# A two-layer encoder trunk on one core: the first norm on rows of x, the residual's transposes between the first products

## What is computed

```python
def rmsnorm(x, g):
    xf = x.astype(F32)
    y = xf * lax.rsqrt(jnp.mean(xf * xf, axis=-1, keepdims=True) + EPS)
    return (y * g.astype(F32)).astype(x.dtype)

# layer 0, its first lines
# u = rmsnorm(x, norm_mix[0])
a_q, a_ckv, i_q, i_k, i_w, b_qkv, b_z, b_beta, b_a = _split(u @ w_in, AB_SIZES)
```

## Time and profile before

| | us |
|---|---|
| median of three runs | 2592.58 |
| lowest and highest | 2591.0, 2593.51 |
| the profiled execution | 2587.56 |
| its span | 2585.8 |
| TensorE busy in it | 2488.4 (96%) |
| VectorE, ScalarE, GpSimd busy | 1549.3, 1008.7, 215.1 |

### The profile page before, as it was taken

How to read it: one execution, slowest core, us unless ns; L and a number is a source line. 1 busy time by engine, 2 the same in 40 slices (tenths; PEclk the granted TensorE clock), 3 DMA queues, 4 the chain that set the end, 5 groups by cost and what they waited for, 6 DMA issues and landing times.

```text
span 2585.8 us, 33956 instructions
## 1 busy us (share of the span) xinstructions
PE 2488.4 (96%) x13076; PEld 1955.7 (76%) x13078; DVE 1549.3 (60%) x2649; ACT 1008.7 (39%) x1816; POOL 215.1 (8%) x243
## 2 busy tenths in 40 slices
PE   7999999998898999999999998998999999999998
PEld 5587777875546788888888786776878888888786
DVE  6379976855544685656543546728576566553444
ACT  4323324545433343333332433428444333333333
POOL 4015533410000000000010000000000000000000
PEclk8999989999999999999999999999999999999999
DMA  5121100000003322222364341110332322336342
GB/s 174 48 74 41 41 25 10 3 34 1 1 25 121 131 74 82 83 80 82 90 225 146 133 137 41 43 39 28 96 114 82 98 66 87 94 100 234 122 159 102
DMA packets 207184, 217.54 MB, mean 84 GB/s; under 512 B 12496, under 2 KB 174304, under 8 KB 203568
## 3 DMA queue, kind: packets, MB, share of 16 engines
q1 hardware_dynamic: 204080, 196.13, 24.4%
q0 software_dynamic: 2944, 19.24, 2.1%
HBM read 172.35 MB, written 42.47 MB: 83 GB/s over the span
## 4 chain that ended last, share of the span: by engine, by line
PE 88%; DVE 6%; ACT 4%; issue 2%; POOL 0%; DVEq 0%; ACTq 0%; POOLq 0%
PE ps L333 24%; PE ps L334 24%; PE ps L335 24%; PE ps L2887 2%; PE ps L2864 1%; PE ps L2875 1%; ACT d_p L1524 1%; DVE met L2012 1%; PE ps L2251 1%; PE ps L2265 1%; PE ps L2260 1%; PE ps L1797 1%; PE ps L2304 1%; PE ps L2228 1%; PE ps L2313 1%
## 5 line engine op out<-in xcount | busy, mean ns | idle before, releaser
L322 DVE TENSOR_TENSOR wlo<-wraw,whi 128x1024 fp32r<-128x1024 f32 x152 | 186.4, 1227 | 370.0 <-ACT whi L316 369.6
L316 ACT ACTIVATE whi<-wraw 128x1024 fp32r<-128x1024 f32 x166 | 175.0, 1055 | 354.3 <-PE ps L335 337.6
L333 PE MATMUL ps<-ahi,whi 128*128 128x512 f32 x704 | 275.3, 391 | 6.5 <-DVE hT L960 4.3
L334 PE MATMUL ps<-alo,whi 128*128 128x512 f32 x704 | 273.9, 389 | 0.0
L335 PE MATMUL ps<-ahi,wlo 128*128 128x512 f32 x704 | 273.9, 389 | 0.0
L333 PE MATMUL ps<-uhi,whi 128*128 128x512 f32 x608 | 244.7, 402 | 8.2 <-DVE ulo L492 4.2
L333 PE MATMUL ps<-q_T,whi 128*128 128x512 f32 x640 | 249.2, 389 | 1.6 <-ACT upr L761 1.6
L335 PE MATMUL ps<-q_T,wlo 128*128 128x512 f32 x640 | 249.0, 389 | 0.0
L334 PE MATMUL ps<-q_T,whi 128*128 128x512 f32 x640 | 249.0, 389 | 0.0
L333 PE MATMUL ps<-q_B,whi 128*128 128x512 f32 x608 | 238.9, 393 | 2.4 <-DVE q_B L492 2.4
L335 PE MATMUL ps<-uhi,wlo 128*128 128x512 f32 x608 | 238.0, 392 | 0.0
(11 more groups left out here) (459 smaller groups left out, 4517.8 us busy)
## 6 DMA issues: line engine op xcount, KB each, us to landing
wraw<-in_ffn_w_down_dram SPq DMA_DIRECT2D x88, 512.0 KB, 3.7
wraw<-in_ffn_w_gate_dram SPq DMA_DIRECT2D x44, 512.0 KB, 4.7
araw<-acts SPq DMA_DIRECT2D x88, 256.0 KB, 3.9
wraw<-in_ab_w_in_dram SPq DMA_DIRECT2D x24, 512.0 KB, 3.8
park<-hT POOLq DMA_DIRECT2D x3, 4096.0 KB, 11.5
wraw<-in_ffn_w_up_dram SPq DMA_DIRECT2D x24, 512.0 KB, 5.2
acts<-sgA SPq DMA_DIRECT2D x12, 1024.0 KB, 4.6
raw<-in_ffn_w_up_dram SPq DMA_DIRECT2D x20, 512.0 KB, 4.0
```

The lines of the kernel that those rows point to most:

```text
L316: nc.scalar.activation(as_raw(whi[:, t.slot, :]), raw, ACT.Copy).then_inc(S("w_high"), 1)
L322: eng.tensor_tensor(as_raw(wlo[:, t.slot, :]), raw, as_raw(whi[:, t.slot, :]).bitcast(F32), ALU.subtract).then_inc(S("w_split"), 1)
L333: nc.tensor.matmul(dst, wh, xh, start=start, stop=False, **kw)
L334: nc.tensor.matmul(dst, wh, xl, start=False, stop=False, **kw)
```

## The change

The norm's factor is now taken from rows, where a token lies on one partition. ScalarE squares each row block as it lands and sums it in the same instruction, then takes the root; VectorE inverts and scales the row block into a second copy (`x_scaled`). TensorE turns the scaled rows too (`scaled`), into banks 4 to 7. ScalarE reads the bank with the gain as its scale and rounds to `uhi` (`high`), VectorE reads bank, gain and `uhi` and writes `ulo` in one instruction (`low`). The sums of squares over partitions, the diagonal and the spreading are gone from this norm.

The raw x is still turned for `hT`: 3 groups ahead of the scaled ones, the other 13 one by one between the three-product steps of tile 1. Twelve pieces are moved by VectorE and the last four by ScalarE, which does this inside `ab_act` behind tile 3's rounding. The scaled groups 3 to 7 and 11 to 15 stand between the products of tile 0. The warm-up has 28 matmuls, and two instead of one behind each of the first three groups. SyncE loads rows 0, 1, the gain, rows 2, 3, weight tile 0, rows 4 to 7, weight tile 1. GpSimd issues the small loads as soon as the masks are made; their scratch place has moved under `hT`, so that piece 6 waits for `masks_ready`. The split of the small columns moves behind tile 3's rounding on ScalarE and VectorE. Parking waits for all 16 raw pieces.

```diff
+            rows(0)
+            rows(1)
             sp_.dma_start(gains[:, 0, :], gain[0], allow_slow_non_contiguous=True).then_inc(S("gain_landed"), 16)
+            rows(2)
+            rows(3)
+            weights(0)
             for b in range(4, NB):
-                sp_.dma_start(xrow[:, b, :], x[0, b * P:(b + 1) * P, :]).then_inc(S("x_landed1"), 16)
+                rows(b)
+            weights(1)
...
+            def raw(g):
...
+                if 3 <= g < 11:
+                    pe.wait_ge(S("x_raw"), g - 1)
+                if 11 <= g < 15:
+                    pe.wait_ge(S("u_ready"), g + 2)
...
+            def scaled(g):
+                h, k = divmod(g, KT)
                 if k == 0:
...
+                    pe.wait_ge(S("x_scaled"), 4 * h + 4)
+                if g >= 4:
+                    pe.wait_ge(S("u_ready"), g - 3)
...
+            busy(pe, 28)
+            for g in range(3):
+                raw(g)
+                busy(pe, 2)
+            for g in range(3):
+                scaled(g)
+            w_ready(pe, t[0])
+            for k in range(KT):
+                part(0, 0, k)
+                if k + 3 < KT:
+                    scaled(k + 3)
+            w_ready(pe, t[1])
+            pe.wait_ge(S("x_raw"), 1)
+            for k in range(KT):
+                part(1, 0, k)
+                raw(3 + k)
+            for g in range(8, 11):
+                scaled(g)
...
+            def square(b):
+                act.wait_ge(S(f"x_landed{b}"), 16)
+                if b:
+                    act.wait_ge(S("x_squared"), b)
+                act.activation(xsq[:, :], xrow[:, b, :], ACT.Square, accum_out=sp[0][:, b:b + 1]).then_inc(S("x_squared"), 1)
+                act.wait_ge(S("x_squared"), b + 1)
+                act.activation(root[:, b:b + 1], sp[0][:, b:b + 1], ACT.Sqrt, scale=1.0 / D,
+                               bias=epsc[:, 0:1]).then_inc(S("x_root"), 1)
...
+            def high(g):
+                act.wait_ge(S("x_s_turned"), g + 1)
+                act.activation(uhi[:, g % KT, rows_of(g // KT)], bank(4 + g % 4), ACT.Identity,
+                               scale=gains[:, 0, g % KT:g % KT + 1]).then_inc(S("nrm_hi"), 1)
...
+            def scale(b):
+                dve.wait_ge(S("x_root"), b + 1)
+                dve.reciprocal(rinv[:, b:b + 1], root[:, b:b + 1]).then_inc(S("x_rinv"), 1)
+                dve.wait_ge(S("x_rinv"), b + 1)
+                dve.tensor_scalar(x_scaled(b), xrow[:, b, :], rinv[:, b:b + 1], None, ALU.mult).then_inc(S("x_scaled"), 1)
...
+                dve.scalar_tensor_tensor(out=ulo[:, k, rows], in0=bank(4 + g % 4), scalar=gains[:, 0, k:k + 1],
+                                         in1=uhi[:, k, rows].bitcast(F32), op0=ALU.mult, op1=ALU.subtract).then_inc(S("u_ready"), 1)
...
+            for b in range(3):
+                scale(b)
+            raw_move_dve(dve, 0)
+            scale(3)
+            w_low(dve, Tile(n_ab))
             dve.wait_ge(S("gain_landed"), 16)
...
+            for g in range(7):
+                low(g)
             w_low(dve, Tile(n_ab + 1))
...
+            low(7)
+            raw_move_dve(dve, 1)
+            raw_move_dve(dve, 2)
+            for b in range(4, NB):
+                raw_move_dve(dve, b - 1)
+                scale(b)
+            for g in range(7, 11):
+                raw_move_dve(dve, g)
+            for g in range(8, 16):
+                low(g)
+            raw_move_dve(dve, 11)
```

More of the change, by code:

```diff
@@ L1046, in busy @@
             for _ in range(n):
-                pe.matmul(bank(7), steady[:, 0:P], steady[:, :], start=True, stop=True)
+                pe.matmul(bank(0), steady[:, 0:P], steady[:, :], start=True, stop=True)
         def load_pe(pe):
[L1051 to L1056, removed]
-                if k == 0:
[L1058 to L1061, removed]
@@ L1063, in sums @@
-            def sums(h):
-                pe.wait_ge(S("x_acc"), 7 * h + 7)
-                row_sums(pe, bank(4 + h), acc_half(h), 4).then_inc(S("x_sums"), 1)
-            pe.wait_ge(S("consts"), 1)
[L1068 to L1077, removed]
@@ new lines, in load_pe @@
+            t = [Tile(n_ab), Tile(n_ab + 1)]
+            def raw(g):
+                h, k = divmod(g, KT)
+                if g == 0:
+                    for b in range(4):
+                        pe.wait_ge(S(f"x_landed{b}"), 16)
+                if g == 8:
+                    for b in range(4, NB):
+                        pe.wait_ge(S(f"x_landed{b}"), 16)
+                if 3 <= g < 11:
+                    pe.wait_ge(S("x_raw"), g - 1)
+                if 11 <= g < 15:
+                    pe.wait_ge(S("u_ready"), g + 2)
+                if g == 15:
+                    pe.wait_ge(S("x_raw"), 12)
+                for b in range(4):
+                    last = pe.transpose(bank(RAW_BANK[g])[:, b * P:(b + 1) * P], xrow[:, 4 * h + b, k * P:(k + 1) * P], ident[:, :])
+                last.then_inc(S("x_turned"), 1)
@@ new lines, in load_pe @@
+            for g in range(8, 11):
+                scaled(g)
+            pe.wait_ge(S("x_raw"), 10)
+            for k in range(KT):
+                last = part(0, 1, k)
+                if k + 3 < KT:
+                    scaled(11 + k)
+            last.then_inc(S("w_used"), 1)
+            pe.wait_ge(S("x_raw"), 11)
+            for k in range(KT):
+                last = part(1, 1, k)
+                if k < 5:
+                    raw(11 + k)
+            last.then_inc(S("w_used"), 1)
+        def load_act(act):
+            def square(b):
[10 more added lines that the diff above has]
+                               scale=gains[:, 0, g % KT:g % KT + 1]).then_inc(S("nrm_hi"), 1)
+            act.sem_inc(S("nrm_sq"), 16)
+            act.sem_inc(S("nrm_root"), 2)
+            act.activation(sp[1][:, 0:1], epsc[:, 0:1], ACT.Sqrt)
+            for b in range(4):
+                square(b)
+            w_high(act, Tile(n_ab))
+            act.wait_ge(S("gain_landed"), 16)
+            for g in range(6):
+                high(g)
+            w_high(act, Tile(n_ab + 1))
+            for g in range(6, 8):
+                high(g)
+            for b in range(4, NB):
+                square(b)
+            for g in range(8, 16):
+                high(g)
```

148 lines of the change are left out of this document (59 added, 89 removed).

## The result

| | before | after |
|---|---|---|
| median of four runs, us | 2593.05 | 2573.99 |
| lowest and highest | 2591.0, 2598.22 | 2570.85, 2575.18 |
| profiled execution | 2587.56 | 2570.85 |
| its span | 2585.8 | 2569.1 |

The ratio is 0.992, with a 95% interval of 0.9904 to 0.9935: the change makes the kernel faster by 0.8%. The forecast, 2578.9 us, lay too high by 4.9 us, and the result stands just under the range that began at 2574.0.

What follows compares the result with a forecast made beforehand. TensorE was taken as the bound: 15.5 + 21.8 + 11.4 + 3.5 + 1.8 = 54.0 us for tile 2's start, against 67.7 us. The 13.7 us shift from 2592.58 us gave median 2578.9 us, range 2574 to 2585 us.

Steps and rivals of the forecast that it cites:

- the mechanism and its place: TensorE's path bounds; the start is worth what brings tile 2's first product forward, from 67.70 to 54.0 us.
- First product, 15.5 us: At the start, warm-up, transposes, scaling and rounding lead to the first product at 15.5 us, 25.8 us earlier.
- Products and groups: Before tile 2, 96 products at 0.227 us take 21.8 us and 26 transpose groups at 0.44 us take 11.4 us.
- Switches, 3.5 us: Between products and transposes before tile 2, 23 rounds cost 0.15 us each, 3.5 us, out of 0 to 4.6 us.
- Waits, 1.8 us: TensorE waits before tile 2: 0.8 us at tile 1's split, 0.8 us before the second half, 0.2 us for the rest.
- the third rival: At the start the clock falls once, or slowed scalings and small gaps add up: 8.7 us less, 2583.9 us; chance 0.18.
- The shift is the same for both: Over the whole kernel, profiled execution and median of timed runs both fall by the start's 13.7 us.
- About 1 us for the spread of the runs: In the forecast range for the whole kernel, the allowance for scatter between runs was about 1 us.
- The second: Before tile 2, switches and waits cost next to nothing: tile 2 at 50.0 us, 17.7 us less, 2574.9 us; chance 0.12.
- The fourth: Clock stays at 1.2 GHz from the first product on: tile 2 at 90.7 us, 23.0 us later, 2615.6 us; chance 0.04.
- The fifth: Parking transfer meets weight loads of tiles 5 to 7; a late load takes the shift back: 2592 us; chance 0.06.

Runs made afterwards that it cites:

- after again: The changed kernel, unchanged, timed in six more runs: median 2571.9 us, ratio 0.9923.
- the doubled groups: The changed kernel with every transpose group that stands between products done twice, 23 groups more: median 2584.62 us, ratio 0.9972.
- before with its clock kept up: The kernel before with extra warm-up matmuls put into TensorE's waits at the start: median 2583.38 us, ratio 0.9972.
- the shorter start: The changed kernel with loads, scalings, splits and copies reordered against its remaining start waits; two sets of six: medians 2570.48 us (0.992) and 2575.21 us (0.9944).

## Why the prediction was right or wrong, step by step

**Right: the mechanism and its place.** TensorE bounds, and the start is worth what brings tile 2 forward. Predicted for tile 2's first product: 54.0 us; measured 52.54 us. Later stages shifted with it.

**First product, 15.5 us.** Measured 14.94 us. The warm-up ended at 9.94 us and not at 10.7 us. From there TensorE's own list leads to the scaled groups at 12.54 us (13.3 predicted), and high and low parts followed (0.69 and 0.75 us). The chain over rows 2 and 3 came out just as long: row 2's square waited for its landing until 8.45 us, row 3's scaling ended at 12.43 us (13.0 predicted). So the prediction had the right chain, and it started 0.76 us earlier than forecast. The warm-up is shorter because its matmuls got faster sooner in this execution: in the three microseconds from 5.0 us on 5, 6 and 7 of them stand, in after again 4, 3 and 4. The granted clock is 1.00 in these rows in both and doesn't tell why. In after again the warm-up took 9.08 us and the first raw group stood at 11.30 us, and in all profiles of the changed kernel's list with 28 or 36 warm-ups the first product followed 5.0 to 5.1 us behind the first raw group.

**Products and groups: right.** 96 products at 0.227 us and 26 groups at 0.44 us; the doubled groups confirm the second price between products.

**Switches, 3.5 us: the term of the sum that failed.** It rested on the timeline around the small transposes, where the first product behind transposes takes 0.34 us to its successor. Of its two parts the first, a step of 0.32 us from product to transposes, doesn't occur: it is 0.23 us here (15.48 to 15.71 us). The second is really there, 0.32 us in the rows above (16.06 to 16.38 us). But the prediction added it to a full 0.44 us for the group, whereas in a round the product starts 0.35 us after the group does (15.71 to 16.06 us). What the product pays more, the group has paid less. A round is 1.13 us, against 0.68 + 0.44 = 1.12 us. For the whole stretch some 0.9 us are left for switches and restarts behind waits: 52.54 - 14.94 - 21.8 - 11.4 - 3.5 us of waits.

**Waits, 1.8 us.** Measured 3.5 us, as step from start to start less the normal step. Before tile 0's seventh and eighth part, around the split of tile 1, 1.3 us (0.8 predicted; the steps 21.12 to 21.66 us and 22.22 to 23.45 us; the first, 0.3 us, is ScalarE's rounding of tile 1 from 19.19 us on, ahead of the seventh high part, which the prediction had left out), before the second half 0.95 us (0.8 predicted). The rest is 1.3 us in place of 0.2 us, but within the 0 to 1.5 us that the prediction allowed: 0.9 us of it at 30.4 to 32.7 us, behind VectorE's scaling of 1.30 us, and 0.3 us at 44.03 us. "Scalings slowed to the 1.22 us of other passes" stood under the third rival; one of eight did so, and one more took 1.13 us. The mistakes in switches (2.6 us too much) and waits (1.7 us too little) have opposite signs, and with the first product's 0.6 us leave the shift 1.5 us too small.

**From the shift to the median: the step that put the number out.** "The shift is the same for both", profile and median, failed; it makes 3.4 of the 4.9 us by which the forecast missed, and the sum the other 1.5 us. With the measured shift alone the forecast would have been 2577.4 us, well inside the range. The profiled execution fell by 16.7 us: 15.2 us of shift, and 1.6 us between the last ScalarE instruction and the end (4.9 against 3.3 us). That last part is not an effect of the new start that I can show: the groups turned twice have 5.0 us there and before with its clock kept up 3.2 us. The median fell by 18.6 us: the median of the three runs of before lay 5.0 us above its profile, that of the four of after 3.1 us above theirs, which makes the other 1.9 us. So 13.7 + 1.5 + 1.6 + 1.9 = 18.7 us, which is the measured 18.6 us within rounding. "About 1 us for the spread of the runs" was far too little for a kernel in which the same work takes 2502 to 2514 us. Over all executions the medians lie 20.3 us apart, 5 to 6 us more than the mark gives; where those come from is open, as said above.

**The rivals.** The second, switches and waits at next to nothing, was right on the switches and wrong on the waits; its 17.7 us lie further from the measured shift than the forecast's 13.7. That its 2574.9 us comes within 0.9 us of the median is luck. The third did not happen: no fall before 350 us. The fourth fell, also with over half of the time in transposes and over 7.6 us of transposes alone. The fifth fell: at 345.6 us, far behind tiles 5 to 7 and the parking transfer, the shift is 15.1 us.

## What to carry to other kernels

Work that only has to be done sometime belongs between products at the rate at which its consumers can take it: together it runs at their speed. Price a switch between kinds of instruction from start to start over a whole round, since a longer step in one place is often a shorter one beside it. Before a gain of a few microseconds is believed or a spread is forecast, cut several profiles at one mark in front of the shared code and compare what comes behind; the mark tells what the edit did, and the lowest run only does so over many executions (those of the shorter start's two sixes lie 4.7 us apart).

## What I had not expected of the hardware

- The same 28 warm-up matmuls took 7.68 to 9.08 us and the same 20 took 6.20 to 6.79 us in different executions, while the granted clock in those rows is 1.00.
- Falls of TensorE's clock come at the same stages in every profiled execution, but with a length that varies; the profiles of a kernel can agree to 0.1 us over 2500 us or differ by over 6 us.
- Groups of four 128x128 f32 transposes among products cost 0.44 us and nothing for the switch, and they did not bring the clock down at 56% of the time, nor in 7.6 us without a product.
- One 128x1024 scaling in eight took 1.30 us in place of 0.75 us. The row of VectorE does not show why, and it is not tied to a row block: after again has it at row block 4 (1.17 us), and with 36 warm-ups none of the last four was slow. GpSimd issues small loads then (four from 29.05 us on), a rival cause that no run varies.
